# First tile of a gMLP and short-conv layer by fp32 row transposes, with set-up steps at other places of the queues

## The chip, the cores and the metric

One Trainium2 chip, all 8 cores. Each core runs the same program on its own prompt sequence (2048 tokens) and on 16 of the 128 sample tokens; the cores exchange nothing. The time is the device time of the slowest core in microseconds (us). A core has TensorE (PE, matrix products), VectorE (DVE), ScalarE (ACT), GpSimd (POOL) and SyncE (SP), which here only issues transfers. Each engine works through its own queue in order.

## The reference, cut to what matters

```python
def rmsnorm(x, g): return x * rsqrt(mean(x*x, -1) + EPS) * g

mod = silu(c) @ w_ada + b_ada                      # 6 vectors of 1024 per sequence
sh1, sc1, gt1, sh2, sc2, gt2 = split(mod, 6)
h = rmsnorm(x, g_mix) * (1 + sc1) + sh1
u, v, B, C, hin = split(h @ w_in)                  # 5 x 512 columns
v = rmsnorm per head of gelu(v)                    # 8 heads of 64
a_out = gelu(u) * (tril(w_s) v + b_s)              # per head, chunks of 128 rows
b_out = B * conv3(C * hin)                         # causal, width 3
x = x + gt1 * (concat(a_out, b_out) @ w_out)
h2 = rmsnorm(x, g_ffn) * (1 + sc2) + sh2
x = x + gt2 * (relu(h2 @ w_ff1)**2 @ w_ff2)
y = rmsnorm(x, g_final)
```

Sizes: model width 1024, inner width 4096. Inputs and outputs are fp32; the large products run in bf16.

## The kernel before, in words

A core's 2048 tokens are 8 tiles of 256 rows. Phase A (token mixing) runs over the tiles t0 to t7, phase B (the MLP) over the same tiles afterwards. Weights arrive as fp32 in device memory and are cast to bf16 by transfers that POOL issues (`ada_dma`, `win_dma`, `ff1_dma`, `ff2_dma`; 1024 KB at the destination each). The program issues them ahead, in this order: pieces 2 and 3 of w_ada, w_in's u, pieces 0 and 1, w_in's v, C, h, B, then pieces 4 and 5, w_out, pieces 6 and 7. Rows of x and the small tables are issued by SP (`load`; line 99 is where nearly every transfer of both queues is issued).

What each engine does is the order in which the program records operations (`S.op`, `S.dma`). A waiting operation holds up everything behind it on its engine; SP's transfers too wait in order.

Steps that the change touches:

- `n_stats(tl, j)`: ACT squares 128 rows of x with a row sum (`Square`), DVE adds eps (line 398), POOL raises to -0.5. `n_mod` multiplies by that and by `g1B`, a copy of the row g_mix*(1+sc1) in all partitions (DVE, bf16 out). `n_tr` transposes it in bf16 on PE (line 438) and ACT copies it out, so that h stands with the model width in partitions.
- `ada_cols(q)`: PE makes 512 columns of `mod` as a column table `modT` (line 350), DVE adds the bias and, for i = 1, forms g_mix*(1+sc1). `ada_bcast(q)`: DVE widens the columns into `col`, PE turns them into broadcast rows with fp32 products (line 374), ACT writes them to `g1B`. The pieces 2 and 3 are sc1.
- `A_u_hold(tl)`: the u product of t0 and t1, kept in PSUM banks until the bias from sh1 is known (`ada_cols(0)`, `ada_cols(1)`, `win_bias("u")`, line 465); `A_u_out` then evicts them, and `A_u(t2, c)` follows. All large products are issued at line 317.
- `v_bias`, `A_v(tl, j)`: the v product and its bias, as a ninth product of 34 rows (`vbK`), then gelu, square, a sum per head (line 521) and the power on POOL. `A_vn` scales v by it and by `gvB` (DVE). `A_spatial` multiplies by the masked w_s (`wmT`) on PE (lines 579 and 583).
- `setup_spatial` prepares the bias table `bsK` and an indicator `indK`: POOL memsets, DVE casts (lines 965 to 970) and two small SP transfers. `setup_spatial_pe` transposes `wst3` (w_s as loaded) on PE (line 1015) and ACT writes `wmT`. Line 1061 is the mask on POOL, `affine_select` over `wst3`.

The SP queue of the front, in order: small tables, x of t0, the two transfers of `setup_spatial`, x of t1 (behind the landing of piece 3), x of t2 (behind w_in's u), `gvB` (behind piece 1), `wst`, then x_s and the conv state (behind w_in's C), x of t3 and t4 (behind w_in's B).

## Time and profile before

| | us |
|---|---|
| median of 3 runs | 787.66 (783.75 to 789.23) |
| the profiled execution, slowest core | 784.98, its span 783.4 |
| spans of the 8 cores in it | 776.2 to 783.4 |
| busy in the span: PE | 721.9 |
| DVE, ACT, POOL | 373.3, 272.5, 141.8 |
| mean granted TensorE clock of the cores | 0.982 to 0.987 of full |

The span runs from the first to the last instruction; the run's time is 1.6 us longer. In the rows below, the number in square brackets is time in which an engine stood still just before a piece of work, with the work that ended the wait. Times are counted from the start of the span of core 4, the slowest.

### The profile page before, as it was taken

The numbers are of one execution on the slowest core, as the hardware profiler recorded it, in microseconds if no ns is written. First come the engines' busy times: TensorE is split into PE (matmuls) and PEld (weight loads), VectorE is DVE, ScalarE is ACT, GpSimd is POOL, SyncE is SP. The second block draws the span as 40 slices with busy tenths as digits, with TensorE's granted clock in tenths as the row PEclk, the third lists the DMA queues.
The fourth block names the chain that finished last, engine by engine and source line by source line (L and its number), as shares of the span: only waits on it lengthen the run. The fifth ranks groups of instructions, "written<-read, shape, count | busy, mean of one in ns | idle before, by whom it ended". The sixth has DMA issues, their size and how long they took to land.

```text
span 783.4 us, 16529 instructions; the slowest of 8 cores (776.2 to 783.4 us)
## 1 busy us (share of the span) xinstructions
PE 721.9 (92%) x5941; PEld 498.7 (64%) x5976; DVE 373.3 (48%) x795; ACT 272.5 (35%) x560; POOL 141.8 (18%) x154
## 2 busy tenths in 40 slices
PE   1468799999999999997999999999999999999996
PEld 0354477767575766843784784774874865865854
DVE  0333667665757675440643444434433543533523
ACT  2234335423332332441441451351441531532511
POOL 5213302434544453110010000000000000000000
PEclk9989799999999999999999999999999999999998
DMA  9999999999998859997110100200200200200001
GB/s 143 186 172 168 185 187 139 172 197 247 194 275 191 201 96 208 179 192 126 67 44 26 70 18 28 82 2 28 82 1 28 82 2 27 82 1 28 28 1 55
DMA packets 46983, 83.03 MB, mean 106 GB/s; under 512 B 2204, under 2 KB 31654, under 8 KB 46902
## 3 DMA queue, kind: packets, MB, share of 16 engines
q0 software_dynamic: 32304, 36.70, 34.1%
q1 hardware_dynamic: 14598, 45.27, 18.4%
q8 instruction: 49, 0.80, 0.4%
q14 instruction: 32, 0.26, 0.1%
HBM read 101.73 MB, written 16.96 MB: 151 GB/s over the span
## 4 chain that ended last, share of the span: by engine, by line
PE 79%; DMA 14%; DVE 2%; issue 2%; ACT 1%; POOL 1%; another core or an unknown queue 0%; DVEq 0%; POOLq 0%; ACTq 0%; SPq 0%
PE ps L317 71%; DMA arena<-w_ff 6%; DMA arena<-w_ada 6%; DMA arena<-w_s 3%; PE ps L438 1%; PE ps L890 1%; ACT arena L322 1%; DVE arena L328 1%; DVE arena L325 1%; PE ps L746 1%; PE ps L583 1%; PE ps L579 1%; POOL arena L99 1%; PE ps L350 1%; PE ps L656 1%
## 5 line engine op out<-in xcount | busy, mean ns | idle before, releaser
L317 PE MATMUL ps<-arena 128*128 128x256 bf16 (+3 forms) x4376 | 635.0, 305 | 10.4 <-DVE arena L325 3.6
L317 PEld LDWEIGHTS ps<-arena 128*128 128x128 bf16 x4408 | 430.1, 98 | 205.0 <-issue 23.1
L325 POOL TENSOR_TENSOR arena<-arena 128x1 f32<-128x1 f32 (+3 forms) x100 | 107.1, 1076 | 597.1 <-DVE arena L398 466.6
L325 DVE TENSOR_TENSOR arena<-arena 128x256 bf16<-128x256 f32 (+8 forms) x354 | 159.5, 459 | 113.6 <-ACT arena L322 102.3
L322 ACT ACTIVATE arena<-ps,arena 128x256 f32<-128x256 f32 (+1 forms) x320 | 147.1, 472 | 137.4 <-PE ps L317 74.3
L322 ACT ACTIVATE arena<-arena 128x256 f32<-128x256 f32 (+4 forms) x101 | 76.8, 772 | 204.9 <-DVE arena L325 143.3
L325 DVE TENSOR_TENSOR arena<-ps,arena 128x512 f32<-128x512 f32 (+6 forms) x98 | 59.4, 610 | 179.4 <-PE ps L317 129.1
L328 DVE SCALAR_TENSOR_TENSOR arena<-arena 128x256 f32<-128x256 f32 (+4 forms) x118 | 96.2, 822 | 22.6 <-POOL arena L325 15.6
L322 ACT ACTIVATE arena<-ps 128x1024 bf16<-128x1024 bf16 (+4 forms) x86 | 50.6, 590 | 158.3 <-PE ps L438 92.1
L328 DVE SCALAR_TENSOR_TENSOR arena<-ps,arena 128x256 bf16<-128x256 f32 (+1 forms) x64 | 31.0, 484 | 23.2 <-PE ps L317 11.2
L890 PE MATMUL ps<-arena 128*128 128x512 bf16 x125 | 28.4, 379 | 5.6 <-DMA arena<-w_ff 4.8
L438 PE MATMUL ps<-arena 128*128 128x128 bf16 x256 | 20.2, 231 | 6.4 <-DVE arena L328 5.8
L890 PEld LDWEIGHTS ps<-arena 128*128 128x128 bf16 x128 | 12.0, 97 | 21.5 <-issue 8.0
L438 PEld LDWEIGHTS ps<-arena 128*128 128x128 bf16 x256 | 17.3, 103 | 9.6 <-issue 7.4
L398 DVE TENSOR_SCALAR arena<-arena 128x1 f32<-128x1 f32 x46 | 7.0, 153 | 33.1 <-ACT arena L322 32.4
L521 DVE TENSOR_REDUCE arena<-arena 128x8 f32<-128x512 f32 x16 | 10.9, 682 | 11.4 <-ACT arena L322 11.4
L350 PE MATMUL ps<-arena 128*128 128x17 bf16 x384 | 11.8, 172 | 4.9 <-DMA arena<-w_ada 4.9
L350 PEld LDWEIGHTS ps<-arena 128*128 128x128 bf16 x384 | 11.6, 98 | 5.7 <-issue 5.3
L99 POOL DMA_DIRECT2D arena<-w_ff x16 | 13.4, 840 | 9.2 <-PE ps L317 7.2
L99 POOL DMA_DIRECT2D arena<-w_ada x12 | 11.3, 941 | 10.8 <-PE ps L350 9.8
L374 PE MATMUL ps<-arena 128*128 128x128 f32 x16 | 4.1, 437 | 8.4 <-DVE arena L995 7.1
L579 PE MATMUL ps<-arena 34*128 34x512 bf16 x16 | 6.6, 412 | 5.0 <-DVE arena L1022 5.0
(86 smaller groups left out, 106.9 us busy)
## 6 DMA issues: line engine op xcount, KB each, us to landing
arena<-x_p SPq DMA_DIRECT2D x32, 512.0 KB, 11.4
arena<-w_ff POOLq DMA_DIRECT2D x16, 1024.0 KB, 36.2
arena<-w_ada POOLq DMA_DIRECT2D x12, 1024.0 KB, 44.4
x_scr<-arena SPq DMA_DIRECT2D x16, 512.0 KB, 9.6
arena<-x_scr SPq DMA_DIRECT2D x16, 512.0 KB, 4.2
y_p<-arena SPq DMA_DIRECT2D x14, 512.0 KB, 2.9
arena<-w_in POOLq DMA_DIRECT2D x5, 1024.0 KB, 64.4
arena<-w_out POOLq DMA_DIRECT2D x2, 1024.0 KB, 88.3
```

The lines of the kernel that those rows point to most:

```text
L99: fn = lambda eng, o=out, i=in_: eng.dma_start(out=o, in_=i)
L317: ins = e.matmul(out, lhsT=l, rhs=r, start=(first and i == 0), stop=(last and i == n - 1))
L322: S.op("act", lambda e: e.activation(out=out, in_=in_, func=func, **kw), reads=reads, writes=writes)
L325: S.op(eng, lambda e: e.tensor_tensor(out=out, in0=in0, in1=in1, op=op), reads=reads, writes=writes)
L328: S.op("dve", lambda e: e.scalar_tensor_tensor(out=out, in0=in0, scalar=scalar, in1=in1, op0=op0, op1=op1), reads=reads, writes=writes)
L350: ins = e.matmul(bk[:, cc * 17:(cc + 1) * 17], lhsT=ff1_v[s][:, k, cc * 128:(cc + 1) * 128], rhs=siluCT3[:, k, :], start=(k == 0), stop=(k ...
L438: ins = e.transpose(psb[:, (k - k0) * 128:(k - k0 + 1) * 128], hb[:, k * 128:(k + 1) * 128], identb)
L521: S.op("dve", lambda e: e.tensor_reduce(out=ss, in_=sqv.rearrange("p (h d) -> p h d", h=8), axis=AX.X, op=ALU.add), reads=[sqv_b], writes= ...
L579: e.matmul(bk[:, :], lhsT=indK[0:34, :], rhs=bsK[0:34, :], start=True, stop=False, skip_group_check=True)
L583: ins = e.matmul(bk[p0:p0 + 64, (h // 2) * 128:(h // 2 + 1) * 128], lhsT=vt[:, h * 64:(h + 1) * 64], rhs=wmT3[:, h, :], start=False, stop= ...
L656: ins = e.matmul(bk[:, gi * 64 + c * 16:gi * 64 + (c + 1) * 16], lhsT=w_in_g[nm][:, k, c * 128:(c + 1) * 128], rhs=hsT3[:, k, 0:16], start ...
L890: ins = e.matmul(bk[:, :], lhsT=f3[:, k, j * 128:(j + 1) * 128], rhs=wff2_v[:, k, n * 512:(n + 1) * 512], start=(k == 0), stop=(k == 31))
```

## The change

For t0 the rows of x are scaled in place by ACT (`first_rows`), transposed as fp32 by PE (`first_tr`, 16 transposes of 128x128 into four banks), and multiplied by the column table at the eviction (`first_scale`, half on DVE, half on ACT). So t0 no longer waits for `g1B`; both `ada_bcast` stand behind it. `setup_spatial` moves from ahead of `ada_cols(2)` to behind `ada_bcast(3)`. On SP, `wst` moves ahead of the x of t2 and waits for w_in's u; `gvB` no longer waits for piece 1. The `affine_select` over `wst3` moves up, between n_stats and n_mod of t2; `n_stats` and `n_mod` of t2 move ahead of `ada_cols(0)`; `setup_spatial_pe` moves from behind `A_v(t1)` to ahead of `ada_cols(1)`. The bias product of `A_v` becomes an operation of its own. The transfers of pieces 6 and 7 are issued after `A_v(t2)`. One tiny Gelu stands behind the two Silu.

```diff
--- before.py
+++ after.py
@@ -510,9 +510,9 @@
         h3, htb = h3_of(tl)
         vg, vgb, _ = vgs[j]
         bk, bkb = next_bank()
-        S.op("pe", mm_group(bk[:, :], [(h3[:, k, j * 128:(j + 1) * 128], w_in_g["v"][:, k, :]) for k in range(8)]
-                            + [(onesK[0:34, :], vbK[0:34, :])]),
-             reads=[htb, win_b["v"], onesK_b, vbK_b], writes=[bkb])
+        S.op("pe", mm_group(bk[:, :], [(h3[:, k, j * 128:(j + 1) * 128], w_in_g["v"][:, k, :]) for k in range(8)], last=False),
+             reads=[htb, win_b["v"]], writes=[bkb])
+        S.op("pe", mm_group(bk[:, :], [(onesK[0:34, :], vbK[0:34, :])], first=False), reads=[onesK_b, vbK_b], writes=[bkb])
         act(vg, bk[:, :], AF.Gelu_apprx_tanh, [bkb], [vgb])
         act(sqv, vg, AF.Square, [vgb], [sqv_b])
         ss, ss_b = new_stat(8)
@@ -973,6 +973,7 @@
 
     act(cS, cS, AF.Silu, [cS_b], [cS_b])
     act(cP, cP, AF.Silu, [cP_b], [cP_b])
+    act(bF[:, 0:1], mhalf[:, 0:1], AF.Gelu_apprx_tanh, [mhalf_b], [bF_b[0]])
     bk, bkb = next_bank()
 
     def tr_c(e, bk=bk):
@@ -985,26 +986,62 @@
     bk2, bk2b = next_bank()
     S.op("pe", lambda e: e.transpose(bk2[:, 0:88], st88, identf[0:88, 0:88]), reads=st88_b + [identf_b], writes=[bk2b])
     S.op("dve", lambda e: e.tensor_copy(out=cst, in_=bk2[:, 0:88]), reads=[bk2b], writes=[cst_b])
-    for j in range(2):
-        n_stats(tA[0], j)
-
-
-    setup_spatial()
+
+    def first_rows(tl):
+        for j in range(2):
+            n_stats(tl, j)
+        for j in range(2):
+            xt, xb, _ = X[tl["x"] + j]
+            rs, rs_b = tl["rs"][j]
+            act(xt, xt, AF.Copy, [xb] + rs_b, [xb], scale=rs)
+
+    XT_BANKS = (5, 6, 7, 2)
+
+    def first_tr(tl):
+        for q, b in enumerate(XT_BANKS):
+            bk, bkb = banks[b]
+
+            def fn(e, bk=bk, q=q):
+                ins = None
+                for kk in range(2):
+                    for j in range(2):
+                        k = 2 * q + kk
+                        ins = e.transpose(bk[:, kk * TILE + j * 128:kk * TILE + (j + 1) * 128], X[tl["x"] + j][0][:, k * 128:(k + 1) * 128], identf)
+                return ins
+            S.op("pe", fn, reads=[X[tl["x"]][1], X[tl["x"] + 1][1], identf_b], writes=[bkb])
+
+    def first_scale(tl, hf):
+        h3, htb = h3_of(tl)
+        m, mb = modT[1]
+        bk, bkb = banks[XT_BANKS[2 * hf + 1]]
+        k0 = 4 * hf + 2
+        tt("dve", h3[:, k0:k0 + 2, 0:TILE], bk.rearrange("p (k t) -> p k t", k=2), m[:, k0:k0 + 2, 16:17].broadcast_to([128, 2, TILE]),
+           ALU.mult, [bkb, mb], [htb])
+        bk, bkb = banks[XT_BANKS[2 * hf]]
+        for kk in range(2):
+            k = 4 * hf + kk
+            act(h3[:, k, 0:TILE], bk[:, kk * TILE:(kk + 1) * TILE], AF.Copy, [bkb, mb], [htb], scale=m[:, k, 16:17])
+
+    ring[0] = (0, 1)
+    first_rows(tA[0])
+
     ada_cols(2)
-    ada_bcast(2, g1B, g1B_b, col, col_b)
+    first_tr(tA[0])
+    first_scale(tA[0], 0)
     S.op("dve", lambda e: e.memset(blk, 0.0), writes=[blk_b])
     S.op("dve", lambda e: e.memset(blk[0:64, 0:1], 1.0), reads=[blk_b], writes=[blk_b])
     S.op("dve", lambda e: e.memset(blk[64:128, 1:2], 1.0), reads=[blk_b], writes=[blk_b])
     ada_cols(3)
+    first_scale(tA[0], 1)
+    ada_bcast(2, g1B, g1B_b, col, col_b)
     ada_bcast(3, g1B, g1B_b, col, col_b)
     q3_in = landed(ff1_b[ADA_SLOT[3]])
-    q1_in = landed(ff1_b[ADA_SLOT[1]])
-    for j in range(2):
-        n_mod(tA[0], j)
+    setup_spatial()
     for q in (4, 5):
         ada_dma(q)
     for n in range(2):
         S.dma("pool", w_out_v[:, :, n * 512:(n + 1) * 512], wout_src[:, :, n * 512:(n + 1) * 512], [], [wout_b[n]], wout_b[n].name)
+
     def setup_spatial_pe():
         for half in range(2):
             bk, bkb = next_bank()
@@ -1033,16 +1070,14 @@
 
     t0, t1, t2, t3 = tA[0:4]
     hold = {0: (3, 4), 1: (5, 6)}
+    for j in range(2):
+        n_load(t1, j, after=[q3_in])
+    load(wst3, w_s.rearrange("h t s -> t h s"), wst_b, "wst", after=[win_b["u"]])
+    for j in range(2):
+        n_load(t2, j)
+    load(gvB, g_v.partition_broadcast(128), [gvB_b], "gvB")
+    A_u_hold(t0, hold[0])
     ring[0] = (0, 1, 2, 7)
-    for j in range(2):
-        n_load(t1, j, after=[q3_in])
-    for j in range(2):
-        n_load(t2, j, after=[win_b["u"]])
-    load(gvB, g_v.partition_broadcast(128), [gvB_b], "gvB", after=[q1_in])
-    load(wst3, w_s.rearrange("h t s -> t h s"), wst_b, "wst")
-    for j in range(2):
-        n_tr(t0, j)
-    A_u_hold(t0, hold[0])
     for j in range(2):
         n_stats(t1, j)
     for j in range(2):
@@ -1050,16 +1085,17 @@
     for j in range(2):
         n_tr(t1, j)
     A_u_hold(t1, hold[1])
+    for j in range(2):
+        n_stats(t2, j)
+    S.op("pool", lambda e: e.affine_select(out=wst3, in_=wst3, compare_op=ALU.is_ge, fill=0.0, base=0,
+                                           pattern=[[0, 8], [-1, 128]], channel_multiplier=1), reads=wst_b, writes=wst_b)
+    for j in range(2):
+        n_mod(t2, j)
     ada_cols(0)
     sh_split(0, shT3, [shT_b], 0, 0)
     for j in range(2):
-        n_stats(t2, j)
-    for j in range(2):
-        n_mod(t2, j)
-    for j in range(2):
         n_tr(t2, j)
-    S.op("pool", lambda e: e.affine_select(out=wst3, in_=wst3, compare_op=ALU.is_ge, fill=0.0, base=0,
-                                           pattern=[[0, 8], [-1, 128]], channel_multiplier=1), reads=wst_b, writes=wst_b)
+    setup_spatial_pe()
     ada_cols(1)
     sh_split(0, shT3, [shT_b], 0, 1)
     win_bias("u")
@@ -1070,8 +1106,6 @@
         sh_split(0, shT3, [shT_b], 32, j)
     for c in range(4):
         A_u(t2, c)
-    for q in (6, 7):
-        ada_dma(q)
     load(xS, x_s.rearrange("t (k n) -> (t k) n", k=8), [xS_b], "xS", after=[win_b["C"]])
     load(scS, sconv.rearrange("t (j n) -> (t j) n", j=8), [scS_b], "scS")
     for j in range(2):
@@ -1084,13 +1118,14 @@
         A_vn(t0, j)
     for j in range(2):
         A_v(t1, j)
-    setup_spatial_pe()
     for j in range(2):
         A_spatial(t0, j)
     for j in range(2):
         A_vn(t1, j)
     for j in range(2):
         A_v(t2, j)
+    for q in (6, 7):
+        ada_dma(q)
     for j in range(2):
         A_spatial(t1, j)
     for j in range(2):
```

## Rows read from the trace of the kernel before

**Rows 1.** The page: busy tenths of PE and the DMA engines, 40 slices.

```profile
PE   1468799999999999997999999999999999999996
...
DMA  9999999999998859997110100200200200200001
```

**Rows 2.** Chain that ended last, 0 to 110 us: start, length, what.

```profile
6.14 44.50 DMA arena<-w_ada
...
51.09 20.74 DMA arena<-w_s
```

**Rows 3.** The same chain after 110 us, its only transfer.

```profile
313.53 44.79 DMA arena<-w_ff
```

**Rows 4.** PE's timeline to 112 us: start, length, line, shape, count, idle.

```profile
29.47 2.04 PE L374 MATMUL ps<-arena 128*128 128x128 f32 x8 [1.34 <-DVE arena L367]
...
37.45 5.81 PE L317 MATMUL ps<-arena 128*128 128x256 bf16 x32 [1.43 <-ACT arena L322]
...
57.91 0.99 PE L465 MATMUL ps<-arena 128*128 128x2 bf16 x32 [1.11 <-DVE arena L325]
...
67.93 8.45 PE L317 MATMUL ps<-arena 128*128 128x512 bf16 x35 [1.94 <-DVE arena L325]
76.31 1.09 PE L1015 MATMUL ps<-arena 128*128 128x128 f32 x8
...
82.70 0.58 PE L579 MATMUL ps<-arena 34*128 34x512 bf16 x1 [4.98 <-DVE arena L1022]
...
92.67 1.75 PE L465 MATMUL ps<-arena 128*128 128x2 bf16 x64
```

**Rows 5.** SP's issues to 100 us: start, length, what.

```profile
24.83 10.44 SPq L99 DMA_DIRECT2D arena<-x_p  x4
...
88.82 2.32 SPq L99 DMA_DIRECT2D arena<-x_p  x4
```

**Rows 6.** Transfers issued at 33.75, 34.7, 50.71, 51.09, 7.93: us to landing.

```profile
arena<-x_p SPq DMA_DIRECT2D x1, 512.0 KB, 9.2
...
arena<-x_p SPq DMA_DIRECT2D x1, 512.0 KB, 10.9
...
arena<-g_v SPq DMA_DIRECT2D x1, 256.0 KB, 9.8
...
arena<-w_s SPq DMA_DIRECT2D x1, 512.0 KB, 20.7
...
arena<-w_in POOLq DMA_DIRECT2D x1, 1024.0 KB, 53.4
```

**Rows 7.** Packets, MB, share: POOL's q0, SP's q1 (62-64 us); q1 (68-70).

```profile
q0 software_dynamic: 249, 0.25, 80.9%
...
q1 hardware_dynamic: 253, 0.13, 31.7%
...
q1 hardware_dynamic: 63, 0.03, 7.7%
```

**Rows 8.** Timelines of ACT (first row) and DVE, 0 to 112 us.

```profile
17.48 1.06 ACT L322 ACTIVATE arena<-arena 128x1024 bf16<-128x1024 f32 x1 [1.24 <-DMA arena<-x_p]
...
20.82 0.44 DVE L965 CAST arena<-arena 2x128 bf16<-2x128 f32 x1 [1.93 <-POOL arena L923]
...
23.67 0.41 DVE L970 CAST arena<-arena 2x512 bf16<-2x512 f32 x1
...
52.31 2.48 DVE L328 SCALAR_TENSOR_TENSOR arena<-arena 128x1024 bf16<-128x1024 f32 x2 [0.69 <-POOL arena L325]
```

**Rows 9.** Groups, shapes kept apart, to 110 us: busy us, mean ns, idle.

```profile
L325 POOL TENSOR_TENSOR arena<-arena 128x8 f32<-128x8 f32 x6 | 9.8, 1646 | 11.3 <-DVE arena L523 11.3
...
L322 ACT ACTIVATE arena<-ps 128x512 f32<-128x512 f32 x8 | 4.8, 597 | 29.4 <-PE ps L374 12.4 <-PE ps L317 10.8 <-DVE arena L325 4.9
...
L325 DVE TENSOR_TENSOR arena<-arena 128x512 f32<-128x512 f32 x6 | 4.1, 686 | 1.9 <-POOL arena L325 1.8
```

**Rows 10.** Window 79 to 82: PE, PEld, DVE, ACT, POOL busy; PEclk, DMA, GB/s.

```profile
79.00:82.00 3.00, 0.00 (x0) 0.00 (x0) 2.20 (x4) 2.54 (x5) 1.17 (x1) 0.57 1.14 167
```

More of the change, by code:

```diff
@@ L1035, in build_nc @@
     hold = {0: (3, 4), 1: (5, 6)}
-    ring[0] = (0, 1, 2, 7)
     for j in range(2):
         n_load(t1, j, after=[q3_in])
+    load(wst3, w_s.rearrange("h t s -> t h s"), wst_b, "wst", after=[win_b["u"]])
     for j in range(2):
-        n_load(t2, j, after=[win_b["u"]])
-    load(gvB, g_v.partition_broadcast(128), [gvB_b], "gvB", after=[q1_in])
-    load(wst3, w_s.rearrange("h t s -> t h s"), wst_b, "wst")
-    for j in range(2):
-        n_tr(t0, j)
+        n_load(t2, j)
+    load(gvB, g_v.partition_broadcast(128), [gvB_b], "gvB")
     A_u_hold(t0, hold[0])
+    ring[0] = (0, 1, 2, 7)
     for j in range(2):
```

## The prediction

> **What bounds the kernel now.** I read the page's slices first. PE is busy to nine tenths from the sixth slice (98 us) on, but for one slice near 360 us, and the DMA engines are full from the start up to 235 us [rows 1]. So what happens ahead of 98 us, where PE has gaps, can move the end; behind it PE works without a break. Then the chain of waits. It starts in a transfer of w_ada [rows 2], passes to the load of w_s (51.09 to 71.83) and from there over the mask on POOL to A_v's powers; the reader is to see that a load that SP issues late is on the path. After 110 us the only transfer in the chain is that of w_ff2 at 313.53 [rows 3]; POOL issues it once the last phase A tile has freed its room, and the DMA share had fallen before, so it moves with PE and gives nothing back. Hence I cost the change up to one mark, the start of `win_bias("C")` at 92.67, behind which both kernels do the same work [rows 4].
>
> In PE's timeline up to the mark the reader is to see three things [rows 4]: the u product of t0 only at 37.45; `win_bias("u")` at 57.91, behind the chain of t2; and the stop of 4.98 us ahead of the first spatial product at 82.70, which the late w_s makes (POOL's powers stand behind its mask).
>
> **What the change takes away.** The stop of 4.98 us goes, if w_s is in by then. The 1.94 us ahead of A_v(t0) goes, since eight products no longer wait for `vbK` [rows 4]. `setup_spatial_pe` (1.09 us for eight transposes and the small product behind them) is moved ahead of `ada_cols(1)`, not removed. The clock: in 79 to 82 PEclk is 0.57, a mixture of the two levels 2.4 and 1.2 GHz, after PE had stopped [rows 10]; without that stop it need not fall there. Splitting A_v's group adds 16 signals and no product, nothing; the tiny Gelu runs while ACT has nothing to do, before x of t0 is in. The later issue of pieces 6 and 7 costs nothing as long as POOL's queue still has a backlog, and it has, the DMA engines being full [rows 1]: their order there is unchanged and pieces 4, 5 and w_out stand ahead. The mask on POOL stands behind t2's powers, so it delays none of them. A_v itself is limited by its own chain afterwards, worked out below.
>
> **What the change adds, first part: x of t1 comes late.** SP works in order, and the two small transfers of `setup_spatial` still stand ahead of x of t1. They now wait for DVE casts that stand behind `ada_bcast(3)`.
> - ACT finishes the second square at 18.6 [rows 8]; two row scalings at about 1.05 each (the same size as that square) end at 20.7.
> - 16 fp32 transposes. The trace has eight in 1.09 us at full clock, 2.2 for 16; the nearest row at the start is eight fp32 records in 2.04 us, 4.1 for 16 [rows 4]. I take 4.1, since the u product too runs at 0.18 us there for 256 columns (5.81 / 32), where 512 columns take 0.24 later (8.45 / 35): 24.9.
> - `ada_cols(3)` 1.0 on PE, as the 32 like products of `win_bias("u")`, 0.5 on DVE, the eviction of half the tile 0.7, `col` 0.4: 27.5. `ada_bcast(2)` 2.04 on PE [rows 4], `col` again 0.4, gaps 0.7: 30.7.
> - `setup_spatial`'s casts ran from 20.82 to 24.08 [rows 8], 3.3 us; at the same pace they end at 34.0.
>
> SP issues x of t1 at about 34.7 instead of 24.83 [rows 5]. The u product of t0 starts at about 32.7 instead of 37.45, but nothing behind it can use that. A row load issued at that time lands after 9.2, the second after 10.9 [rows 6]: 43.8 and 45.9.
>
> **Second part: x of t2 behind w_s.** The load of w_s takes the place ahead of t2's two. How long is its turn in SP's queue? It was issued 0.4 us behind `gvB`, which landed at 50.71 + 9.8 = 60.5, and w_s landed at 51.09 + 20.7 = 71.8 [rows 6]: 11.3 us, beside a full POOL queue. The count of packets explains it: 253 of SP's beside 249 of POOL's in 2 us [rows 7], one for one, although SP's are half as large, and w_s is 1024 pieces of 512 bytes while x's 128 rows are 128 pieces. Two row loads issued together landed 2.7 us apart (33.75 + 9.2, 34.7 + 10.9). Bounds for w_s's turn: nothing (if t2's loads passed it) and 11.3. I take 11.3, the row of the thing itself; between 62 and 64 the packets of w_s fill SP's share and nothing suggests room beside them. So t2's second load lands at L = 45.9 + 11.3 + 2 x 2.5 = 62.2, instead of 45.6.
>
> The Trainium skill, page "DMA: Bandwidth & Descriptors", section "Queues, rings and completion order", says that each engine consumes the descriptors of one ring in order and takes turns between the queues. By that rule t2's rows can't pass w_s, and the sum is the one here; without it L would be near 48 and the first rival holds. The trace agrees as far as it goes: w_s landed 11.3 us behind `gvB`, which had been issued 0.4 us before it.
>
> **From L to the mark.** Square 1.2, eps 0.4 (the first n_mod stands behind the second eps on DVE and needs no more), 2.48 for both n_mod [rows 8], the last n_tr 1.1: it ends at L + 5.2. Then `setup_spatial_pe`, 2.3 at half clock: 7.5; `ada_cols(1)` 1.0 and its DVE steps 1.1: `win_bias("u")` starts at L + 9.6. Before, from there to the end of `v_bias` it was 57.91 to 66.0, 8.1, part of it at half clock; PE now works somewhat longer ahead of it, which I put at -0.6: L + 17.1. A_v(t0) starts at once.
> From there: A_v(t0) and A_v(t1) are 8.4 of PE [rows 4]. The vectors' chain is longer. A_v(t0, 1) ends at 4.2; gelu and square 1.3 (each pass 0.6 [rows 9]), sum 0.8 with its gap, eps 0.2, power 1.65 [rows 9], A_vn 2 x 0.7 [rows 9] end at 9.8; only then may t1's second gelu write the same buffer: 1.3, then 0.9 and 0.2 on DVE, 12.3. DVE still has t0's two evictions and A_vn's four passes of t1, 6 x 0.75: 16.9. The second spatial product of t1 follows, the mark at 17.4. Before it was 92.67 - 67.93 = 24.74.
> Sum: 62.2 + 17.1 + 17.4 = 96.7 against 92.67, +4.0 us. With 784.98 that makes 789.0 for the profiled execution. The median of the runs lies 2.7 above it; on the median it is 787.66 + 4.0 = 791.7. Half of what hides elsewhere (DVE's queue at t0's conv, 0.5 us more) I leave out.
>
> **What else could bind.** w_in's v lands at 7.93 + 53.4 = 61.3 [rows 6]; about 3.5 us more of SP's bytes now go ahead of it, 65, needed at about L + 15. Of C, h and B, the last landed by 88.82, where SP's transfers that wait for it went out [rows 5]; C is needed at 96.7, B 7 us later. x of t3, issued at 88.82, lands within 14 and is needed behind t0's convolution, 96 products of 256 columns or 11 us behind the mark. None of them binds.
>
> **The rivals.**
> 1. *Loads of t2 hidden (not slower).* w_s's turn in the queue costs t2 little. Then PE's chain of t1 decides: x at 45.9, n_mod to 50.1, transposes and eviction to 52.3, u product 5.8 at half clock, `ada_cols(0)` 1.0, n_tr of t2 2.0: 61.1, where the sum has L + 5.2. So L counts as 55.9, and the mark is at 90.4: -2.3, 785.4. It decides from a turn of less than 5 us. For it: SP's packets had thinned out by 68 to 70, 63 in 2 us [rows 7]; the last part of w_s is a tail of few engines. Against it: the semaphore of a load waits for its slowest part.
> 2. *The front is as fast as its weights (faster).* If x of t1 is not late either, v at about 65 is the limit: `v_bias` ends 1.4 later, mark at 65 + 1.4 + 17.4 = 83.8, -8.9, 778.8. It needs `setup_spatial`'s casts to be over by about 25; their place behind two broadcasts speaks against it.
> 3. *The clock (slower still).* PE waits from about 59 to 65 for t2. If it then gets half clock through A_v(t0) and A_v(t1), 36 products of 512 columns take twice 0.21 each: up to 7.7 more on PE, of which the vectors' chain hides 2: +5.5, 797.2. Against it: PE has ten us of work ahead of A_v, and it had got its full clock in the like place before.
>
> **How the numbers follow.** Forecast 791.7, chance 0.55; its own range, from w_s's turn between 7.5 (from `gvB` landed to where its packets are few) and 11.3, the transposes at 2.2 to 4.1, and 1.5 for the rest, is 786.5 to 793.5. Rival 1: 0.27. Rival 2: 0.08. Rival 3: 0.10. The range 782.5 to 797 leaves out rival 2, a bit of rival 1 and of rival 3, under 0.2. About 1%, 7.9 us, is what a measurement can tell from no change: faster than 779.8 only in rival 2, 0.07; slower than 795.5 in most of rival 3, 0.07; within 1% the rest, 0.86.
>
> **What would show it.** In the changed kernel's profile: SP issues x of t1 near 34.7 (step one); t2's two squares on ACT start near 60 and 62, with a wait for a transfer of x_p ahead of them, behind the landing of w_s near 57 (step two); `win_bias("u")` at 71 to 72; no stop of PE between A_v(t1) and the first spatial product over 1.5 us; `win_bias("C")` at 96.7 instead of 92.67. It is wrong if t2's squares start before 56, or if the mark comes ahead of 92.

## The result, and the profile after

| | before | after |
|---|---|---|
| median of 12 runs, us | 786.47 | 794.03 |
| lowest, us | 783.48 | 789.62 |
| ratio after / before, 95% interval | | 1.0082 [1.0062, 1.0102] |
| profiled execution, slowest core | 784.98 | 789.73 |
| spans of its 8 cores, mean | 776.2 to 783.4, 780.6 | 780.4 to 788.2, 785.0 |

The changed kernel is slower by 0.8%: 6.4 us by the ratio, 4.4 in the mean of the eight spans. In some executions of any of the kernels the cores of one die run at a lower clock and take longer, so ratios are taken from the others alone (three of the 12 of after, up to 914 us, are in its median only), and where the profiled execution of a kernel below was of that kind, its stages are those of cores 0 to 3 and marked so.

**Page of the changed kernel.** First its sum line, then the slices of PE, of the granted clock and of the DMA engines.

```profile
PE 725.4 (92%) x5941; PEld 502.2 (64%) x5976; DVE 371.9 (47%) x795; ACT 275.3 (35%) x565; POOL 143.1 (18%) x154
PE   1646899998999999999999999999999999999996
PEclk9866999999899999999999999999999999999999
DMA  9999997999988649999020110200200200200001
```

PE is busy for 3.5 us more than before, for the same count of products (5941 in both traces). Some 1.3 of it are t0's transposes (3.37 in fp32, where the bf16 ones took 2.10 before), and part of the rest ran at the lower clock: the cores' mean is 0.969 to 0.977 instead of 0.982 to 0.987. In the slices two places differ from [rows 1]. In the front PE is busier in slice 2 and idler in 3 and 4, and in the tenth slice (177 to 197 us) it falls to 8, with the clock down in the next one; before, the only such slice behind the front was near 360 us, and that one has gone.

**PE's timeline of the changed kernel up to 107 us, core 0** (start, duration, engine, line, operation, count; in brackets the idle time before it and what ended it); it answers to [rows 4]. Lines left out are marked by dots.

```profile
20.17 3.37 PE L1009 MATMUL ps<-arena 128*128 128x128 f32 x16 [2.22 <-ACT arena L322]
...
30.75 4.94 PE L317 MATMUL ps<-arena 128*128 128x256 bf16 x32
46.62 1.01 PE L438 MATMUL ps<-arena 128*128 128x128 bf16 x8 [10.93 <-DVE arena L328]
...
62.37 1.01 PE L438 MATMUL ps<-arena 128*128 128x128 bf16 x8 [5.73 <-DVE arena L328]
64.92 1.01 PE L438 MATMUL ps<-arena 128*128 128x128 bf16 x8 [1.54 <-DVE arena L325]
65.72 1.91 PE L1052 MATMUL ps<-arena 128*128 128x128 f32 x8
...
70.34 0.99 PE L465 MATMUL ps<-arena 128*128 128x2 bf16 x32 [1.22 <-DVE arena L325]
...
78.35 8.45 PE L317 MATMUL ps<-arena 128*128 128x512 bf16 x35 [0.16 <-issue]
87.11 0.37 PE L579 MATMUL ps<-arena 34*128 34x512 bf16 x1 [0.32 <-issue]
...
96.63 1.76 PE L465 MATMUL ps<-arena 128*128 128x2 bf16 x64
98.25 8.78 PE L317 MATMUL ps<-arena 128*128 128x256 bf16 x64
```

The u product of t0 is 6.7 us earlier and then PE stands still for 10.93 us, because t1 isn't there; it stands still for 5.73 more, because t2 isn't there. `win_bias("u")` comes at 70.34 instead of 57.91. The stop ahead of the first spatial product has gone (0.32 instead of 4.98), and the mark, `win_bias("C")`, is at 96.63.

**Chain of waits of the changed kernel, 0 to 112 us** (start, duration, piece), which answers to [rows 2], and SP's issues, which answer to [rows 5].

```profile
33.58 5.28 SPq L99
38.95 20.12 DMA arena<-x_p
59.51 1.16 ACT arena L322 x2
```

```profile
28.96 2.73 SPq L99 DMA_DIRECT2D arena<-arena  x2
31.78 0.88 SPq L99 DMA_DIRECT2D arena<-x_p  x2
32.75 0.66 SPq L99 DMA_DIRECT2D arena<-w_s  x1
33.58 5.28 SPq L99 DMA_DIRECT2D arena<-x_p  x1
```

Where the load of w_s stood in the chain before, a load of x stands now: t2's rows, in the queue behind w_s, with 20.12 us of transfer. Note the order in which SP issues: the two transfers of `setup_spatial` first, then x of t1, then w_s, then x of t2.

**The second place.** PE's timeline between 190 and 204 us on core 0, and the same stretch on core 2. Line 656 is a small product for the samples (`s_win`, 96 products of 16 columns).

```profile
192.66 2.35 PE L656 MATMUL ps<-arena 128*128 128x16 bf16 x87
198.27 0.39 PE L656 MATMUL ps<-arena 128*128 128x16 bf16 x9 [3.26 <-issue]
```

```profile
193.10 2.57 PE L656 MATMUL ps<-arena 128*128 128x16 bf16 x96
```

On core 0 PE stops for 3.26 us after 87 of the 96, with nothing in the trace that it waits for ("issue"). On core 2 it runs through. Four of the eight cores of after stop there for 2.27 to 3.26 us (a fifth for 0.28), always with 9 products left; none of before's does. On core 0 the clock is low afterwards, as the windows show (length, busy us and count of PE, PEld, DVE, ACT, POOL, then PEclk, DMA share, GB/s):

```profile
198.00:200.00 2.00, 1.73 (x17) 1.29 (x17) 0.62 (x4) 0.39 (x2) 0.00 (x0) 0.50 1.12 314
200.00:203.00 3.00, 3.00 (x16) 2.13 (x15) 1.77 (x7) 0.63 (x2) 0.00 (x0) 0.50 1.11 307
203.00:206.00 3.00, 3.00 (x25) 2.48 (x24) 1.36 (x5) 1.87 (x4) 0.57 (x1) 0.83 1.17 177
```

### The profile page after: what moved, and what is told of

The parts are those of the page before. It is cut to its first block, busy times and chain, and to the rows that moved or that the text cites. A ratio compares the mean times of both kernels' runs of the same rounds, so it can differ in the third digit from the quotient of the medians.

```text
span 788.2 us, 16544 instructions; the slowest of 8 cores (780.4 to 788.2 us)
## 1 busy us (share of the span) xinstructions
PE 725.4 (92%) x5941; PEld 502.2 (64%) x5976; DVE 371.9 (47%) x795; ACT 275.3 (35%) x565; POOL 143.1 (18%) x154
## 4 chain that ended last, share of the span: by engine, by line
PE 73%; DMA 15%; DVE 3%; issue 3%; ACT 2%; SPq 2%; POOL 2%; DVEq 0%; POOLq 0%; ACTq 0%
PE ps L317 67%; DMA arena<-x_p 8%; DMA arena<-w_ff 6%; ACT arena L322 2%; SPq L99 1%; POOL arena L325 1%; DVE arena L325 1%; PE ps L438 1%; DVE arena L328 1%; DMA mod_scr<-arena 1%; PE ps L746 1%; PE ps L583 0%; PE ps L890 0%; PE ps L579 0%; PE ps L465 0%
## 5 line engine op out<-in xcount | busy, mean ns | idle before, releaser
L325 POOL TENSOR_TENSOR arena<-arena 128x1 f32<-128x1 f32 (+3 forms) x100 | 108.7, 1090 | 621.8 <-DVE arena L398 464.5
L322 ACT ACTIVATE arena<-ps,arena 128x256 f32<-128x256 f32 (+1 forms) x324 | 149.1, 472 | 148.5 <-PE ps L317 76.8
L322 ACT ACTIVATE arena<-arena 128x1024 bf16<-128x1024 f32 (+5 forms) x104 | 79.3, 773 | 218.1 <-DVE arena L325 142.9
L328 DVE SCALAR_TENSOR_TENSOR arena<-arena 128x256 f32<-128x256 f32 (+4 forms) x116 | 95.2, 826 | 19.2 <-POOL arena L325 15.3
L322 ACT ACTIVATE arena<-ps 128x16 f32<-128x16 f32 (+4 forms) x84 | 48.5, 580 | 135.6 <-PE ps L438 80.3
L328 DVE SCALAR_TENSOR_TENSOR arena<-ps,arena 128x256 bf16<-128x256 f32 (+1 forms) x64 | 31.0, 484 | 24.7 <-PE ps L317 11.3
L350 PEld LDWEIGHTS ps<-arena 128*128 128x128 bf16 x384 | 11.3, 97 | 7.0 <-issue 6.6
L322 ACT ACTIVATION_READ_ACCUMULATOR arena<-arena 128x1 f32 x51 | 9.6, 189 | 0.0
```

What stands on the lines that cost most here:

```text
L322: S.op("act", lambda e: e.activation(out=out, in_=in_, func=func, **kw), reads=reads, writes=writes)
L325: S.op(eng, lambda e: e.tensor_tensor(out=out, in0=in0, in1=in1, op=op), reads=reads, writes=writes)
L328: S.op("dve", lambda e: e.scalar_tensor_tensor(out=out, in0=in0, scalar=scalar, in1=in1, op0=op0, op1=op1), reads=reads, writes=writes)
L350: ins = e.matmul(bk[:, cc * 17:(cc + 1) * 17], lhsT=ff1_v[s][:, k, cc * 128:(cc + 1) * 128], rhs=siluCT3[:, k, :], start=(k == 0), stop=(k ...
```

## The experiments

All times of stages below are means over eight cores of one profiled execution, or over cores 0 to 3 where marked "0-3" (for the same cores before has 57.5, 90.9 and 369.1, after 70.3, 97.2 and 374.9). An empty last column: no ratio was to be had. "Mark" is the start of `win_bias("C")`. "Stops" counts, of all eight cores, those on which PE stands still for over 1 us inside line 656.

| kernel | win_bias(u) | mark | end of first w_ff2 stage | stops | ratio to before |
|---|---|---|---|---|---|
| before | 57.7 | 91.4 | 370.3 | 0 | 1 |
| after | 70.2 | 97.1 | 374.8 | 4 | 1.0082 |
| e10_after | 70.6 | 97.6 | 377.3 | 7 | 1.0081 |
| e1_x1 (0-3) | 67.3 | 94.3 | 372.7 | 5 | |
| e2_ws (0-3) | 63.8 | 90.4 | 371.6 | 6 | 1.0019 |
| e3_both (0-3) | 60.1 | 86.8 | 364.3 | 3 | |
| e4_unsplit (0-3) | 70.7 | 99.6 | 378.1 | 4 | |
| e5_q67 | 64.0 | 90.9 | 369.3 | 4 | 1.0006 |
| e6_space | 64.1 | 91.2 | 369.2 | 0 | 0.9964 |
| e7_best | 60.7 | 87.5 | 365.7 | 0 | 0.9938 |
| e8_rows | 62.3 | 89.7 | 371.0 | 7 | 1.0004 |
| e9_after_space | 70.8 | 97.8 | 376.8 | 0 | 1.0057 |
| b1_setup | 62.4 | 95.2 | 372.2 | 4 | 1.0029 |
| b2_ws | 63.1 | 95.9 | 373.8 | 3 | 1.0037 |

Theory A: the loss is the front, and in it two terms, `setup_spatial` ahead of t1's load and w_s ahead of t2's. Theory B: a good part of it is the stop at line 656. (The two can both hold; the runs are to give each its size.)

### The front, part by part

**e1_x1** takes `setup_spatial` off the path of SP:

```diff
     q3_in = landed(ff1_b[ADA_SLOT[3]])
-    setup_spatial()
     for q in (4, 5):
@@
     load(gvB, g_v.partition_broadcast(128), [gvB_b], "gvB")
+    setup_spatial()
```

> The changed kernel, with setup_spatial called behind the loads of t1, w_s, t2 and gvB, so that its two SP transfers no longer stand ahead of x of t1; w_s stays ahead of t2. My theory (t1 late, then w_s's turn, then t2): SP issues x of t1 near 25, its second load lands at 35, w_s at 46 to 47, t2's second load at 52, seven us earlier than in the changed kernel, and win_bias(C) starts near 89.5 instead of 96.6: 7 us less than the changed kernel. Rival (only w_s's place matters, x of t1 could wait): the mark stays within 1 us of 96.6. Rival (weights bind): w_in's v holds the mark at 84 to 86 in this and in the next kernels alike.

Measured: x of t1 is issued at 22 to 24, and its squares run from 31 on. But the mark is 94.3, only 2.8 earlier, where 7 were expected. In ACT's timeline of this kernel, core 0:

```profile
31.17 1.05 ACT L322 ACTIVATE arena<-arena 128x1024 bf16<-128x1024 f32 x1
...
53.98 1.06 ACT L322 ACTIVATE arena<-arena 128x1024 bf16<-128x1024 f32 x1 [14.25 <-DMA arena<-x_p]
56.27 1.06 ACT L322 ACTIVATE arena<-arena 128x1024 bf16<-128x1024 f32 x1 [1.14 <-DMA arena<-x_p]
```

t1's square (the first line) is 10 us sooner than in after, where it runs at 41.38, t2's (the last two) only 3: w_s waits for w_in's u, is issued at 32.03, and its turn in the queue comes ahead of t2. The expectation had it issued right behind t1's rows. So, of the two terms, t1's alone buys 2.8 us.

**e2_ws** puts w_s behind t2's rows instead (in SP's order only):

```diff
-    load(wst3, w_s.rearrange("h t s -> t h s"), wst_b, "wst", after=[win_b["u"]])
     for j in range(2):
         n_load(t2, j)
+    load(wst3, w_s.rearrange("h t s -> t h s"), wst_b, "wst", after=[win_b["u"]])
     load(gvB, g_v.partition_broadcast(128), [gvB_b], "gvB")
```

> The changed kernel with w_s loaded behind t2's rows instead of ahead of them, nothing else. My theory (w_s's 1024 pieces take 11 us of SP's queue ahead of t2): t2's second load lands near 48.6 instead of 59.1, w_s near 60. Then the w_s landing binds setup_spatial_pe, which starts near 61 instead of 65.7: the mark at about 92, 4 to 5 us less. Rival (w_s's turn costs little): t2 lands less than 3 us earlier and the mark does not move by more than 1 us.

Measured: mark 90.4, 6.7 earlier than after; ratio 1.0019 [0.9986, 1.0051]. One line's place is worth most of the 0.8%; the size of this ratio is loose, the 6.7 us at the mark are not. The mark is now 0.5 us ahead of before's on the same cores (90.9), and the kernel isn't measurably faster than before. 6 of its 8 cores stop at line 656.

**e3_both** joins the two edits.

```diff
     q3_in = landed(ff1_b[ADA_SLOT[3]])
-    setup_spatial()
@@
-    load(wst3, w_s.rearrange("h t s -> t h s"), wst_b, "wst", after=[win_b["u"]])
     for j in range(2):
         n_load(t2, j)
+    load(wst3, w_s.rearrange("h t s -> t h s"), wst_b, "wst", after=[win_b["u"]])
     load(gvB, g_v.partition_broadcast(128), [gvB_b], "gvB")
+    setup_spatial()
```

> Both edits together: setup_spatial's transfers behind the loads, w_s behind t2's rows. My theory: x of t1 lands by 35, t2 by 41, w_s by 53; then w_ada's piece 1 and w_in's v (61 to 65) bind, A_v(t0) near 67, the mark at 84 to 86, 11 to 12 us less than the changed kernel and 6 us less than the kernel before, 0.8% faster than before. Rival (the vectors' chain or the clock takes it back): mark at 88 or later, no faster than the kernel before.

Measured: mark 86.8 (84 to 86 were expected), 10.3 earlier than after, so the two terms together are 0.8 more than their sum (2.8 + 6.7). Cores 0 to 3 have spans of 773.6 to 776.1. None of them stops at line 656, but three of the other four do, for 1.26 to 3.26 us. The expected 0.8% over the kernel before has no ratio to test it.

**e4_unsplit** goes back to one operation for `A_v` with its bias.

```diff
-        S.op("pe", mm_group(bk[:, :], [(onesK[0:34, :], vbK[0:34, :])], first=False), reads=[onesK_b, vbK_b], writes=[bkb])
+                            + [(onesK[0:34, :], vbK[0:34, :])]),
+             reads=[htb, win_b["v"], onesK_b, vbK_b], writes=[bkb])
```

> The changed kernel with the bias product of A_v back in one operation with the eight others (waits for vbK ahead of all nine). Cost by the first part: PE waits 1.9 us again ahead of A_v(t0), up to 1.8 us more at the mark. It also takes about ten PE instructions out ahead of the place near 195 us where PE stood still about 3 us on several cores at the same instruction (the 88th product of s_win's second group). Theory A (PE's instruction stream is fetched in blocks, and the block's border falls there): the stop moves to another product or goes. Theory B (data or DMA load of that moment): it stays at the 88th product.

Measured: mark 99.6, 2.5 later than after. PE's line on core 0 has the wait back that [rows 4] show at 67.93 (1.94 us there):

```profile
80.79 8.45 PE L317 MATMUL ps<-arena 128*128 128x512 bf16 x35 [1.94 <-DVE arena L325]
```

So the split is a gain of 2.5 us. The stop stays at the same product (9 left). By the expectation that speaks for theory B of that text and against a block's border; but the ten instructions fewer that it counted on don't show in the traces (5976 products and 5976 weight loads on core 1 of both kernels), so the run decides little.

**e8_rows** keeps w_s's place ahead of t2 and changes the shape of its transfer, from 1024 pieces of 512 bytes to 128 rows of 4 KB. The spatial weights are permuted by that; all the rest is computed alike.

```diff
-    load(wst3, w_s.rearrange("h t s -> t h s"), wst_b, "wst", after=[win_b["u"]])
+    load(wst, w_s.rearrange("h (a b) s -> (h a) (b s)", b=8), wst_b, "wst", after=[win_b["u"]])
```

> The changed kernel (w_s ahead of t2, setup_spatial's transfers ahead of t1) with w_s read as one row of 4 KB per partition instead of 8 pieces of 512 bytes: the same bytes in 128 instead of 1024 pieces. The spatial weights are therefore permuted, all work is done. Theory (packets take turns one for one with POOL's queue, so a load costs by its number of pieces): t2's second load lands 7 to 9 us earlier than 59.1, that is near 51, and win_bias(u) starts near 62 to 63 instead of 70, the mark near 89.5. Rival (the load costs by its bytes): t2 lands within 2 us of 59.1 and the mark stays at 97.

Measured: mark 89.7, 7.4 earlier than after, with the same bytes in the same place of the queue. The transfer of w_s, us from issue to landing, in the changed kernel (core 0; 21.6 on core 1) and in this one (core 1):

```profile
arena<-w_s SPq DMA_DIRECT2D x1, 512.0 KB, 22.1
```

```profile
arena<-w_s SPq DMA_DIRECT2D x1, 512.0 KB, 12.7
```

The price of w_s's turn beside POOL's full queue thus goes with its count of pieces, not with its 512 KB. (No run took POOL's queue away, so what many small pieces cost without it is not shown.) Ratio 1.0004 [0.9988, 1.0021]; 7 of 8 cores stop at line 656.

**b1_setup** and **b2_ws** start from the kernel before and make one edit each, the first diff and the second.

```diff
-    setup_spatial()
     ada_cols(2)
@@
     q3_in = landed(ff1_b[ADA_SLOT[3]])
+    setup_spatial()
```

```diff
+    load(wst3, w_s.rearrange("h t s -> t h s"), wst_b, "wst", after=[win_b["u"]])
     for j in range(2):
         n_load(t2, j, after=[win_b["u"]])
     load(gvB, g_v.partition_broadcast(128), [gvB_b], "gvB", after=[q1_in])
-    load(wst3, w_s.rearrange("h t s -> t h s"), wst_b, "wst")
```

> The kernel before with one part of the change: setup_spatial called behind ada_bcast(3). SP's two small transfers then hold x of t1 until about 30 us instead of 24.8. My theory (each us by which x of t1 is late is worth less than one, since ACT reaches t1's squares only at 37): t1's first square starts near 40, the mark moves from 90.9 (median of the cores) to 92 to 94. Rival (t0's earlier h makes up for it): mark within 0.7 us of 90.9. No stop at the 88th product on more than one core.

> The kernel before with another part of the change alone: w_s loaded ahead of t2's rows and behind w_in's u, gvB left behind piece 1. x of t1 is early here, so w_s can go into the gap behind it: w_s lands near 47, t2's second load near 52 instead of 45.6. My theory: win_bias(u) 1 to 3 us later than 57.7, but the stop of 5 us ahead of the first spatial product goes, mark at 85 to 88 instead of 90.9, 3 to 5 us less than before. Rival (any load ahead of t2's costs its full turn): win_bias(u) 6 us or more later, mark at 91 or later, not faster than before.

Measured for b1_setup: mark 95.2, +3.8 (1.2 above the upper end expected); ratio 1.0029 [1.0009, 1.0049]. For b2_ws the expectation fell. I had expected that an earlier w_s would take away the stop of 4.98 us and so bring the mark forward to 85 to 88; it is at 95.9, 4.5 later than before, ratio 1.0037 [1.0014, 1.006]. Its PE timeline, core 5:

```profile
57.76 1.01 PE L438 MATMUL ps<-arena 128*128 128x128 bf16 x8 [7.22 <-DVE arena L328]
...
63.27 0.99 PE L465 MATMUL ps<-arena 128*128 128x2 bf16 x32 [1.11 <-DVE arena L325]
...
74.12 8.66 PE L317 MATMUL ps<-arena 128*128 128x512 bf16 x36 [1.72 <-DVE arena L325]
...
87.73 0.58 PE L579 MATMUL ps<-arena 34*128 34x512 bf16 x1 [3.61 <-ACT arena L322]
```

t2 is late (a wait of 7.22), `win_bias("u")` comes 5.4 later than before in the mean, and 3.61 us of the stop are still there, now with ACT as the releaser. ACT's timeline of the same core shows why (t1's second gelu, then the two copies of `wmT`):

```profile
84.83 0.60 ACT L322 ACTIVATE arena<-ps 128x512 f32<-128x512 f32 x1 [0.91 <-DVE arena L325]
...
86.11 1.27 ACT L322 ACTIVATE arena<-ps 128x512 bf16<-128x512 f32 x2
```

The copies that the spatial product needs stand on ACT behind t1's two gelus, which wait for `A_vn` of t0 on DVE: that is the place of `setup_spatial_pe` behind `A_v(t1)`, not the load. b1_setup says the same with w_s at its old place in the queue. On its core 1 the mask is done at 72.5, well ahead of the first power of A_v at 76.2, and PE still stops:

```profile
85.01 0.37 PE L579 MATMUL ps<-arena 34*128 34x512 bf16 x1 [3.62 <-ACT arena L322]
```

All eight cores of b1 and of b2 stand there for 3.61 or 3.62 us, those of before for 3.62 to 5.15, in the mean 4.51. In every kernel with `setup_spatial_pe` ahead of `ada_cols(1)` it is 0.2 to 0.4, whether w_s comes ahead of t2's rows (after) or behind them (e2_ws), and without the split as well (e4_unsplit). So the early w_s buys at most 0.9 us of the stop and costs 5.4 of front, and what took the rest away is, by these traces, the other place of `setup_spatial_pe`. No run moves that alone.

### The stop at line 656

**e10_after** is the changed kernel once more, without an edit, on the chip of b1, b2 and e9.

> The changed kernel again, on the same chip as the other three, so that they can be compared with it: ratio to the kernel before 1.006 to 1.010, the mark at 97, a stop of 2 to 3 us at the 88th product on half of the cores or more.

Measured: 1.0081 [1.0052, 1.011]; the loss repeats. This time 7 of 8 cores stop for over 1 us, still with 9 left.

**e5_q67** is e2_ws with the issue of pieces 6 and 7 back at its old place, since they are the transfers whose issue moved nearest ahead of 195 us.

```diff
     for c in range(4):
         A_u(t2, c)
+    for q in (6, 7):
+        ada_dma(q)
@@
         A_v(t2, j)
-    for q in (6, 7):
-        ada_dma(q)
```

> Run e2_ws (changed kernel, w_s behind t2's rows) with the transfers of w_ada's pieces 6 and 7 issued at their old place, ahead of x_s. It asks for the second loss: in e2_ws PE passes 118 to 180 us at the same times as the kernel before, but then stands still 2 to 3.5 us at the 88th product of s_win's second group on 7 of 8 cores (0 of 8 before). Theory Q (the DMA queues around 190 us stand differently because pieces 6 and 7 were issued 27 us later): the stops go, and the distance from the fourth ada_cols to the bias row transfer after them falls to 16 to 17 us on all cores. Theory F (PE's own instruction fetch comes behind another engine's, set by the instruction counts): the stops stay on at least 4 of 8 cores. The mark win_bias(C) stays within 1 us of 90.4 in both.

Measured: 4 of 8 still stop, 1.0006 [0.9987, 1.0025]. The pieces' place isn't the cause, or not the whole of it.

**e6_space**, **e7_best** and **e9_after_space** put one empty slot into the list that spreads small work over phase A, between `ada_job(9)` and the dense s_win products, and take one out of those further down. No work is added or taken away: e6 is e2_ws with the slot, e7 is e3_both with it, e9 is after with it.

```diff
         ada_job(9, D1(1)),
+        None,
         lambda: ([s_win(g) for g in range(2, 5)], s_elem1(), s_v1()),
@@
-        None, None,
+        None,
         lambda: ff1_dma(6),
```

> Run e2_ws with one empty slot of the job list moved between ada_job(9) and s_win(2 to 4), so that the two groups of many short products (32 and 96) stand further apart. Theory F (PE reads its instructions in blocks and two such groups close together use them up faster than a block arrives): the stop at the 88th product shrinks to under 1 us or goes, 3 to 5 us less per core that had it. If the stop has to do with the data of that place or with the DMA load alone, it moves with the group and stays 2 to 3 us long.

> Run e3_both (both transfers put back ahead: x of t1 ahead of setup_spatial's, t2 ahead of w_s) with the same empty slot. The mark as in e3_both, 86.7 on undisturbed cores, 4 us ahead of the kernel before; no stop near 190 us. Theory: 3 to 5 us less than the kernel before, ratio 0.994 to 0.997. If w_ff2's transfers bind later (they start when PE frees their room, so I expect not), the gain would shrink to under 2 us.

> The changed kernel itself with the empty slot between ada_job(9) and s_win(2 to 4), nothing else. Splits its loss in two: the front stays (mark near 97), the stop near 195 us goes. Theory F: 3 to 4 us less than the changed kernel, ratio to the kernel before 1.003 to 1.005. If the stop's time is taken back later (w_ff2's landings), the ratio stays at 1.007 or more.

Measured: no core of the three kernels stops. e6 0.9964 [0.9945, 0.9984], 0.55% under e2, which ran on another chip, and 0.42% under e5 on the same one (e5 differs from e2 by the place of two transfers; the intervals don't meet). e9 1.0057 [1.0036, 1.0078] beside e10's 1.0081 on the same chip, 0.24% or some 1.9 us; the intervals overlap, so this single difference is weak. The mean of the eight spans over the executions that the ratios use points the same way: 785.9 in e9 against 787.3 in e10, 778.8 in e6 against 780.2 in e5, 1.4 us in each pair. Part of what the slot saves is lost again further down. e9 reaches the first w_ff2 stage 2.7 us ahead of e10 (344.4 against 347.1), waits there 2.2 us for w_ff2 where e10 waits 0.6 (means of the eight cores), and ends it only 0.6 ahead. e7_best 0.9938 [0.9914, 0.9962], median 780.7 against 785.47: it beats both kernels. PE's line 656 in e9_after_space, core 0, and its mark in e7_best:

```profile
201.38 2.57 PE L656 MATMUL ps<-arena 128*128 128x16 bf16 x96
```

```profile
60.00 0.99 PE L465 MATMUL ps<-arena 128*128 128x2 bf16 x32 [1.22 <-DVE arena L325]
...
87.58 1.75 PE L465 MATMUL ps<-arena 128*128 128x2 bf16 x64
```

What the runs settle: theory A has the larger part. The mark's 5.7 us of lateness is front alone, and e9, where nothing stops, still loses 0.57% of the 0.8%. Theory B's part is some 0.2% here and 0.4 to 0.5% where w_s stands behind t2; its size is less sure than its sign, and the slot also shifts all that stands around it, so the stop's own part isn't isolated. How many cores stop varies from one execution to the next (4 and 7 with the same kernel), and the slowest core sets the time. Open is 0.36% by which e6_space beats the kernel before although its mark is level (91.2 against 91.4): 1.1 us are there by the end of the first w_ff2 stage (369.2 against 370.3), and the mean of the eight spans is 1.4 less over the same executions as above (778.8 against 780.2). The rest of the 2.8 lies in how far the slowest core is behind that mean, and why that is less in e6 was not looked for.

## Why the prediction was right, and where its steps were not

The forecast was 791.7 and within 1%; the median is 794.03 (793.3 without the three executions named above, at the upper end of the range of 786.5 to 793.5 that the forecast had with a chance of 0.55), the ratio 1.0082. It said +4.0 us, and 6.4 were measured. The direction, the place and the two added terms (t1's rows behind `setup_spatial`, t2's behind w_s) held; what took away the stop was misread, and the number at the mark owes something to luck. By its own steps:

- **SP issues x of t1 at 34.7.** 31.78, 2.9 earlier. The mis-sized terms: 16 fp32 transposes took 3.37, not 4.1 (between the two rows, 2.2 and 4.1), and `setup_spatial`'s casts 2.4, not 3.3 (that of line 967 took 0.41, where it had taken 0.99 at its old place). The rest is gaps.
- **t1's second load at 45.9.** 43.6, by the same 2.9 less 0.6.
- **w_s's turn of 11.3.** w_s landed at 32.75 + 22.1 = 54.85, that is 11.3 behind t1's second landing. Exact, and e8_rows shows why it has that size. Rival 1, which needed less than 5, fell.
- **"The stop of 4.98 us [...], which the late w_s makes".** The stop went, as forecast, but for another reason. With w_s in time and nothing else changed (b2_ws) 3.62 us of it stay, and the same with w_s in its old place (b1_setup). The late w_s made at most 0.9 of 4.5; the rest is the place of `setup_spatial_pe`, whose move the prediction priced as a cost of 2.3 us ahead of `ada_cols(1)` and not as the thing that removes the stop.
- **L = 62.2, squares of t2 near 60 and 62.** 57.00 and 59.51, so L is 59.1: the error of the first term carried on.
- **From L to `win_bias("u")`, 9.6.** 11.2. Here a step failed in its mechanism. "The mask on POOL stands behind t2's powers, so it delays none of them" holds for the powers; but I did not ask what DVE does beside the mask, and that is t2's second n_mod. DVE's and POOL's lines on core 0 show it (the first n_mod and the second; then the two powers and the mask):

```profile
60.94 1.28 DVE L328 SCALAR_TENSOR_TENSOR arena<-arena 128x1024 bf16<-128x1024 f32 x1
62.74 2.04 DVE L328 SCALAR_TENSOR_TENSOR arena<-arena 128x1024 bf16<-128x1024 f32 x1 [0.51 <-POOL arena L325]
```

```profile
58.55 0.55 POOL L325 TENSOR_TENSOR arena<-arena 128x1 f32<-128x1 f32 x1 [11.78 <-DVE arena L398]
61.07 1.57 POOL L325 TENSOR_TENSOR arena<-arena 128x1 f32<-128x1 f32 x1 [1.97 <-DVE arena L398]
62.60 1.10 POOL L1090 TENSOR_SCALAR_AFFINE_SELECT arena<-arena 128x1024 f32<-128x1024 f32 x1
```

The second n_mod takes 2.04 instead of 1.28 beside the mask, 0.8 us; and the power takes 1.57 instead of 0.55 beside the first n_mod, so that DVE waits 0.51 for it. That is 1.3 of the 1.6. In e2_ws the mask comes only at 58.77 (core 0), clear of the second n_mod, and that takes 1.28 again:

```profile
54.91 1.28 DVE L328 SCALAR_TENSOR_TENSOR arena<-arena 128x1024 bf16<-128x1024 f32 x1 [0.51 <-POOL arena L325]
```

- **A_v at L + 17.1, the mark 17.4 behind it.** 78.35 is L + 19.2; the mark is 18.3 behind. So L to the mark is 37.5, not 34.5.
- **The mark at 96.7.** 96.63. The number is right by luck: two errors of 3 us cancel, the front too slow by 3, the stretch behind t2 too quick by 3.
- **The reference.** I took before's mark from its slowest core, 92.67; over the eight cores it is 90.3 to 92.7, mean 91.4, and after's is 96.2 to 98.2, mean 97.1. The change cost 5.7 at the mark, not 4.0. On one core an error of 1.3 us in the reference is a third of the difference that was sought.
- **No stop over 1.5 us before the first spatial product.** Right (0.32 and 1.30), and the clock didn't fall in A_v (rival 3 fell: 35 products in 8.45 us, as before). On six of the eight cores it fell behind the mark instead, where the 64 products take 8.8 us (7.15 on six of the cores of before); but those cores of before had their low clock just ahead, in the products of A_v(t2), 5.4 to 6.6 us against 4.4. The sums, 13.2 in after and 12.6 to 13.8 in before, are alike; the loss of clock is moved rather than made.
- **"Behind which both kernels do the same work".** The work is the same, its time is not: PE stops at line 656 on half the cores, 2 to 3.3 us, with half clock behind. Nothing in before's trace stops there, and I had looked at no row beyond 110 us for what an arrival 5 us later would meet.
- **The transfer of w_ff2 "gives nothing back".** It does. The same stage, line 890, first in before on core 4, then in after on core 4 (this view ends at 376 us):

```profile
358.46 3.61 PE L890 MATMUL ps<-arena 128*128 128x512 bf16 x16 [1.75 <-DMA arena<-w_ff]
...
364.66 3.61 PE L890 MATMUL ps<-arena 128*128 128x512 bf16 x15 [2.59 <-DMA arena<-w_ff]
```

```profile
368.27 3.61 PE L890 MATMUL ps<-arena 128*128 128x512 bf16 x16 [1.35 <-DMA arena<-w_ff]
...
374.24 2.10 PE L890 MATMUL ps<-arena 128*128 128x512 bf16 x9 [1.46 <-DMA arena<-w_ff]
```

Over the eight cores this stage takes 32.5 us before and 30.0 after; on core 0 of after it has only 0.42 us of such a wait. It starts 6.9 later than before and ends 4.5 later. My argument was that the transfer moves with PE. Its issue does: the last three transfers of w_ff2 are issued 6.9 later in the mean of the cores. But the median of their times from issue to landing is 43.8 us, not 47.2, so they land only about 3.5 later. Why they ran faster stays open.

The sum then reads, in means of eight cores: +5.7 at the mark, +6.9 at the start of that stage (half of the cores have stopped by then, for 2.9 us and the half clock behind it), +4.5 at its end, and +4.4 in the spans.

## What to carry to other kernels

A load with many small pieces, put in a busy queue ahead of what is needed next, costs its count of pieces, even when it is itself needed soon; put it behind, or give it long rows. A stop can have a second cause right behind the one that the trace names: b2_ws took the named one away and 3.6 of 4.5 us stayed, so ask what would end the wait next before counting the whole of it as won. Price an edit of the front from the mean over all cores, since the slowest one is a reference with an error of its own. And where a front moves by some us, look in the trace for dense runs of tiny instructions further down: an arrival at another time can meet a stop there that the old one did not, and an empty slot of schedule is a cheap probe for it.

## What the runs showed of the hardware

**Pieces against a competing queue.** In the changed kernel, 46 to 48 us, while w_s is on its way (core 0), and in e8_rows (core 1) in the same stretch: packets of each queue, MB, share of the engines. A packet of the profile is here one piece: 0.13 MB in 250 are 512 bytes each.

```profile
q0 software_dynamic: 245, 0.25, 80.4%
q1 hardware_dynamic: 250, 0.13, 31.9%
```

```profile
q1 hardware_dynamic: 117, 0.45, 69.2%
q0 software_dynamic: 111, 0.11, 42.5%
```

One for one in both, 250 to 245 and 117 to 111. With pieces of 512 bytes SP moves 0.13 MB in 2 us, with rows of 4 KB 0.45. The Trainium skill, page "DMA: Bandwidth & Descriptors", section "Queues, rings and completion order", says that an engine takes turns between queues packet by packet. Its packet is a bundle of several descriptors, so counts of one piece for one fit it if the bundles of both queues are alike in number, which no run here shows. That a transfer's price beside a full queue follows its pieces is what e8_rows adds (the mark 7.4 us earlier).

**DVE and POOL.** The two slow instructions above lie beside each other's work. The second n_mod of t2 takes 2.03 or 2.04 us on all cores of after, e8_rows and b2_ws, where the mask lies beside it, and 1.28 or 1.29 on all cores of e2_ws, e3_both and e6_space, where the mask comes later. The Trainium skill, page "SBUF — State Buffer", section "SBUF: two separate sides", says that a VectorE operation with two inputs in SBUF and a GpSimd operation that reads SBUF exclude each other for the whole instruction. The durations fit (2.04 and 1.57 us instead of 1.28 and 0.55). The runs show that work side by side lengthens both; that one engine shuts the other out is the page's reading, and no run shows it.

**PE without instructions.** The stop has the releaser "issue" and lies at the 88th product of 96 in every stopping core of the after kernels and at the 90th in b1 and b2; one empty slot ahead of the products takes it away. The page's queues of instructions (the last columns are packets, MB, share) are the candidate:

```profile
q8 instruction: 49, 0.80, 0.4%
q14 instruction: 32, 0.26, 0.1%
```

The page doesn't say whose they are. If q8 is PE's, its 49 packets of 16 KB stand for PE's 11,917 records of products and weight loads, 243 to a packet; line 656 gets through its 192 in 2.57 us, so a packet's worth lasts about 3.3 us there (an estimate from these three numbers), with the DMA engines full. In after, on the four cores that stop, a packet of q14 comes first and q8's 2 to 3 us behind it (core 0: 193 and 196); on the other four q8's comes at 191 to 192, ahead of q14's or in the same us, and it does so on all cores of before (core 0: 185 and 188). But which of the two is first isn't the whole of it: core 0 of e4_unsplit has q14's first (193 and 195) and runs through.

What holds throughout is the time of q8's packet. On all 56 core traces with a stop, short ones too, PE goes on 2.3 to 3.5 us behind the start of the us in which that packet begins (core 0 of after: 196 and 198.27). In the eleven kernels without the empty slot a core stops when the packet begins 2.8 us or less ahead of the time at which the product after the stop was due by the pace of the others, and runs through when it begins 2.7 us or more ahead. In e6_space the packet comes at 185 to 192 and the dense products start only at 193.2 to 196.8. So late instructions are the likely cause, not a shown one: it's a coincidence in time on every core, and no run moved the packet alone. What decides when it comes was not tried. The Trainium skill, page "Runtime: NRT & Kernel Launch", section "Instruction fetch mechanics", has the fetch of 16 KB blocks as mostly hidden, behind the pace at which instructions are issued. The size agrees with q8's; if the cause is the likely one, it was not hidden here, in a stretch of 192 instructions in 2.57 us.
